# A two-block sequence model on one core: weight splits, statistics and gates of the gating stage in another order

## The reference, cut to what matters

```python
z = gelu(h @ w_in + b_in)            # h: 256 x 1024, w_in: 1024 x 4096
u, v = split(z, 2)                   # 2048 columns each
v = layernorm(v, ln_g, ln_b)         # over the 2048 columns of a token
s = einsum('gij,bnjgc->bnigc', w_s * mask, v) + b_s   # 16 groups of 128 columns
y = (u * s) @ w_out                  # 2048 x 1024
```

## Time and profile before

| | us |
|---|---|
| median of 3 runs | 1210.64 (1207.9 to 1211.09) |
| the profiled execution | 1208.81 |
| its span in the trace | 1206.1 |
| PE busy in the span | 1106.9 |
| DVE busy | 722.3 |
| ACT busy | 560.7 |
| mean granted TensorE clock | 0.971 of full speed |

### The profile page before, as it was taken

The page is one execution under the profiler, slowest core; times in us unless marked ns, Lnnn a source line. Parts: engine busy times, 40 slices in busy tenths (PEclk is TensorE's granted clock), DMA queues, the critical chain, the costliest instruction groups (busy, mean ns, idle before and its releaser), DMA issues.

```text
span 1206.1 us, 20762 instructions
## 1 busy us (share of the span) xinstructions
PE 1106.9 (92%) x8770; PEld 1072.0 (89%) x8770; DVE 722.3 (60%) x963; ACT 560.7 (46%) x697; POOL 28.6 (2%) x24
## 2 busy tenths in 40 slices
PE   5896788999999998799999998998779999999997
PEld 5886678999999788799999998997768999999997
DVE  2665535754456776567655565758976647644554
ACT  3446324544443644434544435799453415443441
POOL 0103210000000000000000000000000000000000
PEclk8898889999999999999999999999889999999999
DMA  9243112655575364445656544513200024655521
GB/s 292 90 139 107 51 35 71 210 178 186 190 282 174 105 210 140 143 156 160 209 175 205 176 174 127 170 36 112 99 2 1 1 93 167 230 176 176 189 87 35
DMA packets 116959, 167.51 MB, mean 139 GB/s; under 512 B 5792, under 2 KB 97568, under 8 KB 116512
## 3 DMA queue, kind: packets, MB, share of 16 engines
q1 hardware_dynamic: 115184, 166.18, 42.3%
q10 hardware_dynamic: 1712, 0.43, 0.2%
HBM read 165.55 MB, written 1.05 MB: 138 GB/s over the span
## 4 chain that ended last, share of the span: by engine, by line
PE 72%; DVE 15%; ACT 7%; issue 4%; DMA 1%; SPq 0%; DVEq 0%; ACTq 0%
PE bank L1831 20%; PE bank L1833 20%; PE bank L1832 19%; DVE sb_w_low L1134 4%; ACT sb_w_high L618 4%; PE bank L2260 1%; PE bank L2337 1%; PE bank L1967 1%; DVE sb_arena L1204 1%; DMA sb_constants<-in_constants 1%; PE bank L1974 1%; DVE sb_arena L1691 1%; DVE sb_state L1688 1%; PE bank L2325 1%; ACT sb_arena L953 1%
## 5 line engine op out<-in xcount | busy, mean ns | idle before, releaser
L1134 DVE TENSOR_TENSOR sb_w_low<-sb_raw,sb_w_high 128x2048 fp32r<-128x2048 f32 x150 | 344.9, 2303 | 296.2 <-ACT sb_w_high L618 296.1
L1831 PE MATMUL bank<-sb_act_high,sb_w_low 128*128 128x256 f32 x1376 | 398.4, 290 | 25.2 <-DVE sb_arena L1533 5.3
L618 ACT ACTIVATE sb_w_high<-sb_raw 128x2048 fp32r<-128x2048 f32 x150 | 285.7, 1910 | 269.4 <-PE bank L1833 269.3
L1833 PE MATMUL bank<-sb_act_high,sb_w_high 128*128 128x256 f32 x1376 | 393.6, 286 | 0.0
L1832 PE MATMUL bank<-sb_act_low,sb_w_high 128*128 128x256 f32 x1376 | 391.4, 284 | 0.0
L1831 PEld LDWEIGHTS bank<-sb_act_high,sb_w_low 128*128 128x128 f32 x1376 | 264.2, 192 | 30.0 <-DVE sb_arena L1193 6.6
L1832 PEld LDWEIGHTS bank<-sb_act_low,sb_w_high 128*128 128x128 f32 x1376 | 266.5, 194 | 0.3 <-issue 0.2
L1831 PE MATMUL bank<-sb_hidden_high,sb_w_low 128*128 128x256 f32 x896 | 255.3, 285 | 9.0 <-DVE sb_hidden_low L1528 9.0
L1833 PEld LDWEIGHTS bank<-sb_act_high,sb_w_high 128*128 128x128 f32 x1376 | 263.3, 191 | 0.0
L1833 PE MATMUL bank<-sb_hidden_high,sb_w_high 128*128 128x256 f32 x896 | 254.3, 284 | 0.0
L1832 PE MATMUL bank<-sb_hidden_low,sb_w_high 128*128 128x256 f32 x896 | 252.2, 281 | 0.0
(11 more groups left out here) (337 smaller groups left out, 1144.1 us busy)
## 6 DMA issues: line engine op xcount, KB each, us to landing
sb_raw<-in_ffn_w SPq DMA_DIRECT2D x64, 1024.0 KB, 5.3
sb_raw<-in_w_up SPq DMA_DIRECT2D x16, 1024.0 KB, 5.3
sb_raw<-in_w_down SPq DMA_DIRECT2D x16, 1024.0 KB, 5.1
sb_raw<-in_sgu_w_in SPq DMA_DIRECT2D x16, 1024.0 KB, 5.3
sb_raw<-in_rwkv_w_rkv SPq DMA_DIRECT2D x12, 1024.0 KB, 5.6
sb_raw<-in_w_in SPq DMA_DIRECT2D x10, 1024.0 KB, 7.6
sb_raw<-in_sgu_w_out SPq DMA_DIRECT2D x8, 1024.0 KB, 4.9
sb_raw<-in_w_out SPq DMA_DIRECT2D x4, 1024.0 KB, 5.2
```

The lines of the kernel that those rows point to most:

```text
L618: nc.scalar.activation(whi[s][:], raw[s][:], ACT.Copy).then_inc(hi_done, 1)
L1134: nc.vector.tensor_tensor(wlo[s][:], raw[s][:], f32(whi[s][:]), ALU.subtract).then_inc(lo_done, 1)
L1831: nc.tensor.matmul(dst, l_lo, r_hi, start=start, stop=False, **kw)
L1833: return nc.tensor.matmul(dst, l_hi, r_hi, start=False, stop=stop, **kw)
```

## The change

Four things. (1) DVE: `low` runs one unit behind the evictions. The eviction of c is now followed by `low(11 + c)`, and `low(19)` stands alone behind the loop. The closing of the v statistics comes behind the eviction of c = 0, the normalisation behind c = 1, `final_norm` behind c = 2 to 5, gates 0 and 1 behind c = 5 and 6. (2) ACT: Ln and Exp of the variance come behind c = 1, the rounded copies of gates 0 and 1 behind c = 5 and 6. (3) PE: `row_sums(2)` and `(3)` stand ahead of U unit c = 2, `spatial(0)` and `(1)` ahead of c = 4 and 5. (4) The folds over eight feature tiles, two in this stage and one in each FFN, are three additions of 1024, 512 and 256 numbers per partition in place of one `tensor_reduce` of 2048.

```diff
@@ ACT
-            log_exp()
-            act.wait_ge(v_stat, 1)
-            rsqrt_of_sums(SG.rs, SG.mv[:, :, 1:2], 1.0, LN_EPS).then_inc(v_stat, 1)
...
             for c in range(8):
-                if c == 6:
-                    gated_high(0)
                 act.wait_ge(u_raw, c + 1)
                 for t in range(2):
                     nc.scalar.activation(SG.U[:, 2 * c + t, :], SG.U[:, 2 * c + t, :], ACT.Gelu,
                                          bias=vcol("b_in_u", 2 * c + t)).then_inc(u_act, 1)
                 high(U_SGU + 12 + c)
+                if c == 1:
+                    log_exp()
+                    act.wait_ge(v_stat, 1)
+                    rsqrt_of_sums(SG.rs, SG.mv[:, :, 1:2], 1.0, LN_EPS).then_inc(v_stat, 1)
+                if c in (5, 6):
+                    gated_high(c - 5)
             log_exp()
             for q in range(1, 8):
-                gated_high(q)
+                if q > 1:
+                    gated_high(q)
@@ DVE
+        def halved(sq, dst):
+            for n in (4, 2):
+                chain.add(nc.vector.tensor_tensor(sq[:, 0:n, :], sq[:, 0:n, :], sq[:, n:2 * n, :], ALU.add))
+                chain.settle()
+            return nc.vector.tensor_tensor(dst, sq[:, 0, :], sq[:, 1, :], ALU.add)
...
-            nc.vector.tensor_reduce(FB.ss, FB.sq.rearrange("p k t -> p t k"), AX_X, ALU.add).then_inc(sq_folded, 1)
+            halved(FB.sq, FB.ss).then_inc(sq_folded, 1)
...
-                nc.vector.tensor_reduce(SG.ss[v], SG.sq[v].rearrange("p k t -> p t k"), AX_X, ALU.add)\
-                    .then_inc(x_folded, 1)
+                halved(SG.sq[v], SG.ss[v]).then_inc(x_folded, 1)
...
-                low(U_SGU + 12 + c)
-                if c < 4:
-                    final_norm(2 * c)
-                    final_norm(2 * c + 1)
+                if c == 0:
+                    statistics(3)
+                    aggregate()
+                else:
+
+                    low(U_SGU + 11 + c)
+                if c == 1:
+                    normalise_values()
                 if c in (2, 3):
                     row_sums(c)
+                if 2 <= c < 6:
+                    final_norm(2 * c - 4)
+                    final_norm(2 * c - 3)
                 if c == 5:
                     dve.wait_ge(t_done, 4)
-                    gate(0)
+                if c in (5, 6):
+                    gate(c - 5)
+            low(U_SGU + 19)
             for q in range(1, 8):
-                gate(q)
+                if q > 1:
+                    gate(q)
                 if q <= 4 or (q <= 6 and on["ffn2"]):
                     low(U_SGO + 3 + q)
@@ PE
-                if c == 7:
-                    row_sums(2)
-                    row_sums(3)
...
             for c in range(8):
-                if c >= 6:
+                if c == 2:
+                    row_sums(2)
+                    row_sums(3)
+                if c in (4, 5):
                     pe.wait_ge(vn_done, 2)
-                    spatial(c - 6)
+                    spatial(c - 4)
                 if c >= 2:
                     pe.wait_ge(u_raw, c - 1)
```

More of the change, by code:

```diff
@@ L1501, in _, with aggregate, normalise_values @@
                     row_sums(g - 1)
[L1502 to L1510, removed]
+            def aggregate():
+                chain.settle()
+                for m in range(CH):
+                    last = nc.vector.bn_aggr(SG.mv[:, m, :], SG.stats[:, m, :, :].rearrange("p a b -> p (a b)"))
+                last.then_inc(v_stat, 1)
+            def normalise_values():
+                dve.wait_ge(v_stat, 2)
+                for m in range(CH):
+                    nc.vector.tensor_scalar(SG.V[:, m, :], SG.V[:, m, :], SG.mv[:, m, 0:1], SG.rs[:, m, :], ALU.subtract,
+                                            ALU.mult).then_inc(vn_done, 1)
             def gate(q):
```

## The result

| | before | changed |
|---|---|---|
| median of 4 runs, us | 1210.62 (1207.90 to 1211.09) | 1188.36 (1188.26 to 1189.99) |
| ratio | | 0.9827 (95%: 0.9815 to 0.9839) |
| the profiled execution, us | 1208.81 | 1189.99 |
| its span | 1206.1 | 1188.2 |

The forecast was 1190.3 with a range of 1187 to 1196. The medians lie 22.3 us apart, the ratio's interval allows 19.5 to 22.4, and the sum was 19.4.

What follows compares the result with a forecast made beforehand. PE bounds the kernel but waits in the gating stage, mostly through DVE's order. 18.6 us there plus 0.8 in the V units, 19.4, off 1208.81 gives 1189.4, off the median 1191.2; the middle is 1190.3, range 1187 to 1196.

Steps and rivals of the forecast that it cites:

- PE's waits go: Gating stage: DVE's instruction order causes nearly all PE waits; reordering removes them, 18.6 us plus 0.8 in the V units.
- 19.4 us off: Whole gain: 18.6 us from the end of the V units to spatial(3), plus 0.8 us of the V units.
- the 61.6 us: PE from the V units' end to spatial(3) without waits: seven units, two row sums, three spatial-and-unit pairs; 80.21 before.
- The circle: U units: eviction, Gelu, high, low, final_norm, next eviction; 6.47 us per unit instead of 5.77, DVE's idle 2.79 goes.
- First evictions: Start of U units: statistics and normalisation no longer precede eviction 0; the 2.29 us wait goes, slack 2.2 us.
- point 4: row_sums(3)'s wait of 0.6 us for the shift of row_sums(1) goes, as the shift is long done two U units later.
- The normalisation: DVE's normalisation of v, behind c = 1, ends at 461.3; spatial(0) needs it at 464.8, slack 3.5 us.
- the slower end: Rival: PE held at U unit c = 4 by late normalised v; 27 us late makes it slower, about 1214; chance 0.02.
- Gates: Gated units: gate 1's hidden_low at 490.7, due 496.1, slack 5.4 us; gate 2's chain has slack 0.1 us.
- The clock: Second gated unit: the 7.16 us wait lowers PE's granted clock, so that unit takes 7.86 us, some 2.0 more.
- The table switch: ACT's table load takes 1.28 us; the skill's 2.66 would cut the normalisation's slack to 2.1, the sum unchanged.
- The folds: Three additions take 2.34 to 2.5 us against 3.85: 0.8 us on PE in the V units, nothing in the FFNs.

Runs made afterwards that it cites:

- the stage's folds back: Changed kernel with the gating stage's two folds done by one tensor_reduce each again: median 1191.45 us, ratio 0.9846, stage 150.57 us.
- folds alone: Kernel before with only the five folds made three additions each: median 1206.04 us, ratio 0.9978, stage 166.05 us.
- the filled gap: Kernel before with 52 unused matmuls in PE's gap ahead of the second gated unit: median 1207.57 us, ratio 0.9985, stage 166.82 us.
- gate 1 back: Changed kernel with gate 1 and its rounded copy behind low(19) and high(19) again: median 1192.46 us, ratio 0.9862, stage 151.70 us.
- the splits alone: Kernel before with only DVE's weight splits (low) moved one unit behind the evictions of u: median 1197.03 us, ratio 0.9908, stage 157.82 us.
- statistics back: Changed kernel with last statistics, closing, Ln, Exp and normalisation ahead of the first eviction and Gelu again: median 1194.39 us, ratio 0.9865, stage 153.19 us.
- splits not behind: Changed kernel with low(12+c) straight behind eviction c again (behind the statistics for c = 0): median 1203.12 us, ratio 0.9948, stage 163.01 us.

## Why the prediction was right

**PE's waits go.** Right, all of them, and none took their place. The step "19.4 us off" measured 19.5 in the stage, but two of its terms were mis-sized and make up for each other. The V units gave 1.27 us instead of 0.8, because the first fold is waited for too, which the sum put at nothing (shown above by the PEld rows and by the stage's folds back). The stretch of 80.21 us became 61.96 (440.57 to 502.53), so it gave 18.25 us instead of 18.6: behind the row sums the first matmul stands 0.52 us ahead of the next (453.39 to 453.91) and not 0.12, in both kernels, and the 61.6 us that were to remain had left that out. So close an agreement is in part luck.

**The circle.** Right, and it weighs more than my list suggests: taken back out of the changed kernel it costs 13.7 us, put alone into the old one it gives 11.0. The 7.16 us that the view of waits books on gate 1 were mostly the circle's arrears; gate 1's own place is worth 2.4 in the changed kernel. The parts don't add up, since each wait is what is left of a lateness after the waits ahead of it.

**First evictions.** The slack of 2.2 us held (eviction over at 451.2, PE past the row sums at 453.4), and undoing the step costs 2.4 us and 1.5 more by the clock. The 0.6 us of point 4 go with the folds alone already; no run moves the row sums, or the `spatial` pairs, by themselves.

**The normalisation.** Forecast until 461.3, it ended at 461.0; `spatial(0)`, forecast at 464.8, started at 465.3. The rival that PE is held up there, and with it the slower end, didn't come: DVE's new wait of 2.17 us lies inside the slack.

**Gates.** `hidden_low` of gate 1 forecast at 490.7, measured 491.1. Gate 2's `hidden_low` was ready at 503.29 for a unit that starts at 503.34, near the slack of 0.1 us, and no wait came of it.

**The clock.** Right in size: 2.0 us forecast, 2.0 us by the filled gap. What I missed is that gaps a third as long can cost nearly as much (1.5 us behind 2.12 us, below).

**The table switch.** The measurement decides against the larger price of the Trainium skill ("ScalarE: Activation LUTs", What ACT_TABLE_LOAD costs): Ln starts 0.02 us behind a load of 1.28, so the switch costs 1.3 us here and not 2.66. The time before the load holds no drain either: it starts 0.02 us behind the end of `high` (454.66 and 1.90 us long).

**The folds.** 2.41 us (403.06 to 405.47) against 2.34 to 2.5 worked out; 1.25 us in the stage where 0.8 were forecast; in the FFNs worth nothing, as forecast. The rule of the Trainium skill ("VectorE: DVE Perf Modes", Rules for kernel authors) to make the number of chained instructions small is outweighed by its other one, that `tensor_reduce` is the slowest of them.

**The time itself.** The median fell 2.8 us more than the stage, and more than the forecast had. Only the profiled executions show their stages. Between those two the time fell 18.8 us: 19.5 in the stage, less the 1.6 us by which the first mixer and FFN2 with RWKV came out longer, and 0.9 us outside the span. The rest of the 22.3 is where these two executions lie among the others, the one 1.8 us below its median, the other 1.6 us above. In which stages the others differ isn't shown. Stages that no edit changes would suffice: over all profiled executions the first mixer takes 201.7 to 205.6 us and FFN2 with RWKV 447.8 to 449.2.

## What to carry to other kernels

Where one engine evicts for another, put what waits for a third engine one round behind the eviction, and look at the whole circle before blaming the instruction at which the arrears come due. Sum such a change on the engine that is to become the bound, as a timetable with a slack for each hand-over, and let the list of idle times only check it. Every wait of two microseconds or more on TensorE should be priced with 0 to 2.7 us of lower clock behind it, the range that these runs show. And the list of PE's waits is not whole: a wait that shows only in the weight loads was worth 0.4 us here.

## What the runs showed of the hardware

Behind idle times of 2.1 to 4 us on PE the granted clock sometimes falls and sometimes doesn't. It stayed at 1.00 behind 2.10 us (gate 1 back) and behind 2.29 us (before, at 457.94, and the splits alone). It fell to 0.77 over the next unit behind 2.12 us (the splits alone) and to 0.72 behind 2.12 us (statistics back) and behind 2.14 us (folds alone), to 0.64 behind 2.95 us and 0.79 behind 3.96 us (splits not behind), against 0.71 behind 7.16 us. So the loss is not in proportion to the gap: 2.65 us behind 2.95 us of idle time, 2.0 behind 7.16 and 1.5 behind 7.15 (folds alone). What decides between equal gaps these runs don't show.

Nor does the clock always fall in the gap. Behind the three gaps of 2.12 to 2.14 us the first matmuls still start 0.12 us apart, the pace of full clock, for 1.1 to 1.4 us. Only then do they start 0.21 us apart, for about 3.3 us, and then 0.12 us apart again. Behind 2.95, 3.96, 7.15 and 7.16 us they start 0.21 us apart at once.

The first mixer, which no edit here touched, ran in 201.7 to 202.7 us in some profiled executions and in 204.5 to 205.6 in others. The slice from 25 to 75 us shows a granted clock of 0.88 in the changed kernel's profile (202.6) and of 0.85 with gate 1 back (205.2):

```profile
25.00:75.00 50.00, 44.78 (x326) 44.11 (x326) 28.67 (x57) 19.96 (x29) 4.79 (x2) 0.88 0.37 110
```

```profile
25.00:75.00 50.00, 44.73 (x320) 44.17 (x321) 26.39 (x52) 19.95 (x29) 4.79 (x2) 0.85 0.35 106
```

In the same 50 us one gets 326 matmuls done and the other 320. The 2 to 4 us between the two groups are one part of the spread of each kernel's times.
